# Branch stages of a first block run beside the next branch's projections, and modulation products moved into the merges

## What is computed

```python
# first block: four branches, merged
y_fox = attention(rms(q), rms(k), v, with a forget bias)         # 16 heads of 64
y_lru = rg_lru(proj("lru_x"), proj("lru_g"))                     # conv, gates, scan, gelu gate
y_sb  = stick_breaking_attention(q, k, v)                        # 16 heads of 64
y_mem = mem_attention(rms(q), rms(mem @ w_k), mem @ w_v)         # 4 heads of 256
gates = sigmoid(proj("gates") + b_gate)
mixed = sum_n gates_n * (y_n @ w_branch_n);  x = x + mixed @ w_out
# second block, each layer i
mod  = silu(c)     @ w_ada[i] + b_ada[i]                         # 6 vectors: shift, scale, gate, twice
modc = silu(c_ctx) @ w_ada[i] + b_ada[i]
h = modulate(rmsnorm(x, g1), sh1, sc1)                           # and the same for the context
ya, yb, yc = neighbourhood_attn, diff_attn, gmlp                 # layer 0: for x and for the context
m = ga * (ya @ w0) + gb * (yb @ w1) + gc * (yc @ w2)
x = x + gt1 * (m @ w_out);  then a mixture of 16 experts
```

## Time and profile before

| what | us |
|---|---|
| median of 3 runs (3232.24 to 3244.42) | 3238.53 |
| the profiled execution's own time | 3241.71 |
| its span, first to last instruction | 3239.9 |
| PE busy in it | 2658.2 |
| the stages fox, lru, sb projections, sb, memory projections together | 360.0 |
| the merge of the first block, the merge of layer 0 | 192.0, 199.1 |
| na_x, na_ctx, da_x of layer 0 together | 152.2 |

### The profile page before, as it was taken

The page is one execution under the profiler, slowest core; times in us unless marked ns, Lnnn a source line. Parts: engine busy times, 40 slices in busy tenths (PEclk is TensorE's granted clock), DMA queues, the critical chain, the costliest instruction groups (busy, mean ns, idle before and its releaser), DMA issues. The chain is left out here.

```text
span 3239.9 us, 36546 instructions
## 1 busy us (share of the span) xinstructions
PE 2658.2 (82%) x14364; PEld 1796.3 (55%) x14364; DVE 1169.5 (36%) x1596; ACT 882.3 (27%) x1314; POOL 39.9 (1%) x36
## 2 busy tenths in 40 slices
PE   6887898998998787889977778887887896787876
PEld 5666687998996464668753222223664894222222
DVE  4446544655753334344432001103444552000001
ACT  3344433544442232322221000002233432000001
POOL 0100000000000000000000000000000001000000
PEclk8888998999998898889978999998897997999999
DMA  4463532453542333112215999996211343999996
GB/s 154 157 257 113 198 130 92 178 185 123 188 159 91 150 136 130 50 69 100 85 46 224 404 405 407 403 414 260 78 52 50 142 165 147 413 410 409 411 410 269
DMA packets 92935, 669.19 MB, mean 207 GB/s; under 512 B 10320, under 2 KB 10496, under 8 KB 12800
## 3 DMA queue, kind: packets, MB, share of 16 engines
q1 hardware_dynamic: 90256, 654.67, 51.6%
q0 software_dynamic: 2272, 11.52, 1.0%
q10 hardware_dynamic: 272, 1.05, 0.1%
HBM read 666.13 MB, written 1.06 MB: 206 GB/s over the span
## 5 line engine op out<-in xcount | busy, mean ns | idle before, releaser
L1860 PE MATMUL ps<-ring,WK 128*64 128x512 f32 x3072 | 731.0, 605 | 171.2 <-DMA ring<-in_stream 147.1
L424 PE MATMUL ps<-A,piece_hi 128*128 128x256 f32 (+1 forms) x1952 | 618.5, 317 | 97.7 <-DVEq L358 33.1
L376 DVE TENSOR_TENSOR ring_lo<-ring,piece_hi 128x1024 fp32r<-128x1024 f32 x378 | 459.3, 1220 | 450.4 <-ACT piece_hi L369 449.3
L425 PE MATMUL ps<-A,piece_hi 128*128 128x256 f32 (+1 forms) x1952 | 612.5, 314 | 0.0
L426 PE MATMUL ps<-A,ring_lo 128*128 128x256 f32 (+1 forms) x1952 | 611.7, 313 | 0.0
L1860 PEld LDWEIGHTS ps<-ring,WK 128*64 128x64 f32 x3072 | 194.5, 137 | 674.2 <-DMA ring<-in_stream 371.9
L424 PEld LDWEIGHTS ps<-A,piece_hi 128*128 128x128 f32 x1952 | 384.7, 197 | 129.3 <-issue 59.2
L369 ACT ACTIVATE piece_hi<-ring 128x1024 fp32r<-128x1024 f32 x378 | 388.2, 1053 | 223.8 <-DVEq L450 131.9
L425 PEld LDWEIGHTS ps<-A,piece_hi 128*128 128x128 f32 x1952 | 385.6, 198 | 17.2
L426 PEld LDWEIGHTS ps<-A,ring_lo 128*128 128x128 f32 x1952 | 384.9, 197 | 18.1
L1980 DVE TENSOR_TENSOR WK<-WK,ps 128x512 f32<-128x512 f32 x32 | 22.0, 688 | 636.7 <-PE ps L1860 636.7
(11 more groups left out here) (252 smaller groups left out, 2447.6 us busy)
## 6 DMA issues: line engine op xcount, KB each, us to landing
ring<-in_stream SPq DMA_DIRECT2D x621, 1024.0 KB, 7.7
WK<-in_na_bias POOLq DMA_DIRECT2D x2, 2048.0 KB, 7.8
WK<-cum_scratch POOLq DMA_DIRECT2D x1, 2048.0 KB, 9.7
const<-in_const SPq DMA_DIRECT2D x1, 1267.0 KB, 11.7
WK<-in_x SPq DMA_DIRECT2D x1, 1024.0 KB, 5.4
WK<-in_mem SPq DMA_DIRECT2D x1, 1024.0 KB, 9.1
WK<-cum_scratch POOLq DMA_DIRECT2D x1, 1024.0 KB, 14.9
WK<-in_lru_w POOLq DMA_DIRECT2D x1, 1024.0 KB, 5.1
```

The costliest lines, as they stand in the source:

```text
L376: nc.vector.tensor_tensor(ring_lo[:, slot, at:at + PIECE], ring[:, slot, at:at + PIECE], f32(piece_hi[:, j, :]), ALU.subtract).then_inc(lo ...
L424: nc.tensor.matmul(out_, l[0], r[0], start=first, stop=False)
L425: nc.tensor.matmul(out_, l[0], r[1], start=False, stop=False)
L1860: last = nc.tensor.matmul(ps[64 * n:64 * n + 64, bank, :], lhs, piece[:, n * 512:n * 512 + 512], start=(k == 0), stop=(k == DC - 1))
```

## The change

**First block.** One projection bank (or a piece of v) stands behind each step of a round. The fox rounds carry the 16 banks of lru_x and lru_g; the recurrence carries the 24 pieces of the sb projections; the sb rounds carry the 16 banks of the memory branch's k and q; the stage of the sb projections is gone, with a barrier. The projections in rounds take PSUM banks 6 and 7 by turns (`set_ring`). The fox product moves from bank 6 to bank 4, the exponentials of round r + 1 stand behind the copy of round r, DVE's `probs(r + 1)` behind the split of a piece. The conv is done in the lru stage as before; Gelu is one operation over all 2048 columns.

**Modulation.** The groups leave the attentions. Each of the six is cut in two halves of 8 raw pieces, and a half stands in a merge, between the four banks of gates and the four banks of products: in halves 1 to 6 of the first block's merge, in all six of layer 0's. The merge uses banks 0 to 5, the modulation banks 6 and 7. The merges are written out, without a loop.

The diff, cut to its core:

```diff
+ADA_HALF = 8
+ADA_MERGE = {0: (1, 2, 3, 4, 5, 6), 1: (0, 1, 2, 3, 4, 5)}
@@ fox_pe
             scores(0)
             scores(1)
             for r in range(HEADS // 2):
+                turn(r)
+                also(2 * r)
+                product(r)
+                also(2 * r + 1)
                 if r + 2 < HEADS // 2:
                     scores(r + 2)
-                turn(r)
-                product(r)
-                after(r)
@@ fox_act
             for r in range(HEADS // 2):
-                if r + 1 < HEADS // 2:
-                    exps(r + 1)
                 act.wait_ge(att_turned, CREDIT + r + 1)
                 act.wait_ge(att_y, CREDIT + r)
                 nc.scalar.activation(fox_pt, ps[:, 4:6, 0:TRI], ACT.Copy).then_inc(att_copied, 1)
+                if r + 1 < HEADS // 2:
+                    exps(r + 1)
+                also(2 * r)
                 act.wait_ge(att_y, CREDIT + r + 1)
-                nc.scalar.activation(YT[:, 0, r, :], ps[:, 6, 0:T], ACT.Copy).then_inc(att_saved, 1)
-                after(r)
+                nc.scalar.activation(YT[:, 0, r, :], ps[:, 4, 0:T], ACT.Copy).then_inc(att_saved, 1)
+                also(2 * r + 1)
@@ sb_pe
             for r in range(SB_ROUNDS):
                 turn(r)
+                mem_piece_pe(pe, cur, 2 * r)
+                product(r)
+                mem_piece_pe(pe, cur, 2 * r + 1)
                 if r + 2 < SB_ROUNDS:
                     scores(r + 2)
-                product(r)
-                after(r)
@@ lru_pe
-            for c in range(DC):
-                pe.wait_ge(lru_xc, c + 1)
-                bank_parts(pe, cur, [... gates of chunk c ...])
+            for i in range(24):
+                sb_piece_pe(pe, cur, i)
+                if i < DC:
+                    if i == 0:
+                        pe.wait_ge(loads, 16 * LOADS["lru_w"])
+                    pe.wait_ge(lru_xc, i + 1)
+                    bank_parts(pe, cur, [(P, g * T, T, [(LW[:, g, i, :], LXC[:, i, :])]) for g in range(2)])
@@ lru_dve
+            for i in range(24):
+                if i < DC:
+                    lru_conv_dve(dve, steps, i)
...
+                sb_piece_read(dve, "dve", cur, i)
@@ merge_pe
                 for h in range(2):
+                    at = 2 * i + h
                     fm_banks(pe, cur, in_a()(n), n, 4)
+                    if ada is not None and ada_half(ada, at) is not None:
+                        ada_half_pe(pe, cur, ada, ada_half(ada, at))
+                    if ada is not None and ada_full_before(ada, at) is not None:
+                        ada_turn_pe(pe, 3 * ada + ada_full_before(ada, at) // 2)
                     if h == 0:
                         pe.wait_ge(y_lo, cur.base("y") + 1 + i)
                     fm_banks(pe, cur, lambda k: (yh[:, k, :], yl[:, k, :]), n, 4, kc)
@@ merge_dve, in a half
                     skip_fm(dve, cur, 4)
+                    if ada is not None and ada_half(ada, 2 * i + h) is not None:
+                        past_raw(dve, cur, ADA_HALF)
+                        if ada_half(ada, 2 * i + h) % 2 == 1:
+                            ada_rows_dve(dve, cur, ada, ada_half(ada, 2 * i + h))
@@
+        def ada_half_pe(pe, cur, layer, half):
...
+            for k in range(4 * (half % 2), 4 * (half % 2) + 4):
+                for q in range(4):
+                    if q % 2 == 0:
+                        piece = raw_piece(pe, cur)
+                        behind = cur.p - 1 - ADA_PIECE[layer, half]
+                        if behind < 4:
+                            pe.wait_ge(bank_free[cur.bank(cur.g - 4 + behind)], cur.bank_use(1, cur.g - 4 + behind))
+                    last = nc.tensor.matmul(ps[32 * q:32 * q + 32, b, :], CS[:, k, :], piece[:, ...], ...)
+                    if (k, q) == (DC - 1, 3):
+                        last.then_inc(ada_full, 1)
+                    elif q % 2 == 1:
+                        raw_used(last, cur)
@@ the program of PE; those of ACT and DVE alike
+            cur.set_ring((6, 7))
+            fox_pe(pe, cur, lambda i: fm_banks(pe, cur, in_a()(T), T, 1))
             barrier(pe, cur)
-            fm_banks(pe, cur, in_a()(T), T, 2 * DC)
+            cur.set_ring(range(NB))
             lru_pe(pe, cur)
             barrier(pe, cur)
-            qk_pe(pe, cur)
-            v_pe(pe, cur)
+            cur.set_ring((6, 7))
+            sb_pe(pe, cur)
             barrier(pe, cur)
-            sb_pe(pe, cur, ada_with_pe(pe, cur, "sb"))
-            barrier(pe, cur)
-            qk_pe(pe, cur, 0, T)
+            cur.set_ring(range(NB))
             head_norm_pe(pe, cur, mem_norm, between=lambda: v_pe(pe, cur, T))
```

More of the change, by code:

```diff
@@ L109, with merge_stretches @@
 RAW[PIECES:] = True
+ADA_HALF = 8
+ADA_MERGE = {0: (1, 2, 3, 4, 5, 6), 1: (0, 1, 2, 3, 4, 5)}
 ADA_PIECE = {}
[L112 to L122, removed]
+def merge_stretches(layer, halves, pieces):
+    out, k = [], 0
+    for h in range(halves):
+        out.append(4)
+        if h in ADA_MERGE[layer]:
+            out.append((layer, k))
+            k += 1
+        out.append(pieces - 4)
+    return out
+_at, _half = 0, {0: 8, 1: 6}
+for _n in ([(6 + 4 + 6 + 6) * 4] + merge_stretches(0, 8, _half[0]) + [BLOCK_PIECES - 22 * 4 - 8 * _half[0], 8 * 4]
+           + merge_stretches(1, 6, _half[1]) + [8, -EXPERTS * EXPERT_PIECES, MIX_PIECES, -EXPERTS * EXPERT_PIECES]):
+    if isinstance(_n, tuple):
+        ADA_PIECE[_n] = _at
+        _n = -ADA_HALF
+    RAW[_at:_at + abs(_n)] = _n < 0
+    assert _n > 0 or _n % 8 == 0
+    _at += abs(_n)
 assert _at == PIECES
@@ L136, in __init__ @@
         self.g = 0
+        self.places = []
+        self.ring = list(range(NB))
+        self.turn = 0
+        self.uses = [0] * NB
         self.i = None
@@ L1088, in fox_dve @@
             maxima(0)
+            probs(0)
             for r in range(HEADS // 2):
@@ L1091, in fox_dve @@
                     maxima(r + 1)
-                probs(r)
-                after(r)
+                also(2 * r)
+                if r + 1 < HEADS // 2:
+                    probs(r + 1)
+                also(2 * r + 1)
             fox_counts(cur)
@@ L1202, in sb_dve, with weights @@
                 nc.vector.memset(SB_B[r][:, :, SB - 1:SB], 0.0)
-            for r in range(SB_ROUNDS):
+            def weights(r):
                 W = SB_W[r % 3]
@@ new lines, in sb_piece_read, with op @@
+        def sb_piece_read(eng, who, cur, i):
+            if i < 2 * DC:
+                dst, scale = ((QT, HD ** -0.5), (KT, 1.0))[i // DC]
+                copies(eng, who, cur, lambda j: dst[:, j, :], 1, T, scale, first=i % DC)
+            elif i % 4 < 3:
+                next_piece(eng, cur)
+            else:
+                h = (i - 2 * DC) // 4
+                for j in range(TT):
+                    def op(bank, j=j):
+                        to = VT[:, j, h * 512:(h + 1) * 512]
+                        if who == "act":
+                            return nc.scalar.activation(to, bank, ACT.Copy)
+                        return nc.vector.tensor_copy(to, bank)
+                    read_bank(eng, cur, who == ("act", "dve")[j], op, piece=(j == TT - 1))
@@ L1286, in lru_dve @@
-            steps(nc.vector.tensor_tensor(LY, LXC[:, :, :], LG[:, :, :], ALU.mult))
-        def merge_loop(eng, cur, branches, kc, one_branch, steps=None, per=0):
-            if 2 * (4 + kc // 2) % (2 * R) == 0:
-                with loop(eng, cur, branches, pieces=2 * (4 + kc // 2), banks=16, steps=steps, steps_per=per) as i:
-                    one_branch(i)
-            else:
-                for i in range(branches):
-                    one_branch(i)
+            flat = lambda x: x.rearrange("p a t -> p (a t)")
@@ L1561, in gmod_dve, with ada_full_before @@
+        def ada_full_before(layer, at):
+            half = ada_half(layer, at - 1)
+            return half if half is not None and half % 2 == 1 else None
         def gmod_dve(dve, steps, g, which):
```

481 lines of the change are left out of this document (249 added, 232 removed).

## The result

| | us |
|---|---|
| before, median of 4 runs in the same comparison | 3235.39 (3227.95 to 3244.42) |
| after, median of 4 runs | 3287.71 (3281.58 to 3291.4) |
| ratio, with its 95% interval | 1.0159 (1.0127 to 1.0191) |
| span of the profiled execution, before and after | 3239.9, 3287.3 |

The changed kernel is slower by 1.6%, about 52 us. The forecast was 3293 us.

What follows compares the result with a forecast made beforehand. PE was taken to bound the kernel where full, chains elsewhere. The profiled 3241.7 - 65.5 (five stages) - 28 (layer 0's attentions) + 148 (merges) = 3296, lying 3.2 over the median, so 3293 us; range 3254 to 3324.

Steps and rivals of the forecast that it cites:

- The five stages: Fox to the memory projections: 294.5 us against 360.0, a gain of 65.5 (bounds 40 to 82).
- Fox: Fox stage: a chain through DVE's split sets rounds of 9.6 us, above PE's 8.5; stage 85 us.
- Lru: Lru stage with the sb projections: 75 us of PE plus 10.2 of waits and tail, 85 us (bounds 79 and 98).
- Layer 0's attentions: na_x, na_ctx and da_x lose their modulation: 11.3, 8.5 and 8.3 us, a gain of 28 (24 to 31).
- The merges: Both merges: 12 modulation halves at 9.95 + 2.2 us, plus 2 for exposed turns, a loss of 148 us.
- the 2 us for exposed turns: Merges: the turn of a finished group fits into the wait except once in each merge, 2 us for two.
- adds no work: Merges: writing the loop out adds no work to a full PE and was counted as nothing.
- Inside a half: Each merge half: PE idles 2.1 us for a landing, then 4.05 before products, which start 9.95 us after the gates.
- my term for the clock: Merges: lower granted clock after idle waits, 2.2 us per half (0 to 3.5), 26 us in all.
- Rival (a): Merges: the clock stays up, 12 x 2.2 us less, 3267 us, still slower; chance 0.18.
- Rival (b): Merges: the stream keeps up, a half costs only 3.64 us, total 3191 us, faster; chance 0.08.
- Rival (c): Fox, lru and sb: interleaved split, read and attention wait for each other, +13, +13 and +8, 3327 us; chance 0.12.

Runs made afterwards that it cites:

- e5_spread_fox: `e1_spread` with DVE's `probs` of the next round ahead of the split in fox; 3230.28 us, ratio 0.9988 to the kernel before.
- e4_fill: Changed kernel plus 28 unread products of 256 columns on PE between each half's modulation and its products; 3272.44 us.
- e6_none: Changed kernel without modulation products and their stream pieces, biases standing in, so part of the computation is left out; 3137.81 us.
- e7_lead: `e5_spread_fox` with one more piece split ahead behind the first three raw pairs of a half; 3192.24 us, ratio 0.9878 to the kernel before.
- e2_short_lead: `e1_spread`, but a raw piece counts as one of the three split ahead, as in the changed kernel; 3324.40 us.
- e1_spread: Changed kernel with two raw modulation pieces (one slot) behind every two merge banks, splits allowed to run past them; 3231.75 us.
- e3_four: Changed kernel with four raw pieces behind the gates and four behind the products, splits ahead as in `e1_spread`; 3231.14 us.
- e8_written_out: The kernel before, with only its first merge written out instead of looped; 3220.47 us, ratio 0.9974.

## Why the prediction was right

The time (3287.7 for 3293), the sign and the mechanism held. By its steps:

- **The five stages.** Forecast 65.5, measured 69.7. Fox 80.3 for 85: the round was 8.91 for 9.6, as the handovers and the bank's read that I estimated overlap in part; that the chain and not PE sets it is shown by `e5_spread_fox`. Lru 86.2 for 85, sb 79.5 for 79, memory 44.3 for 45.5. In lru two misses cancel: PE is busy 77.8 us where 75 were counted, and idles 8.4 where the waits were put at 10.2.
- **Layer 0's attentions.** 26.9 for 28: na_x 10.1, na_ctx 7.8, da_x 9.0.
- **The merges.** Loss 150 for 148; that these agree to 2 us is luck. The halves cost 12.7 and 13.1 us, not 12.15, 9 us more in all. Against that the loop gave 5 back, where "adds no work" to a full PE was taken for "nothing": that PE is busy 185.5 of 192.0 us meant that 6.5 were open, and I did not ask what released it there. And the 2 us for exposed turns are already in the 12.7 and 13.1.
- **Inside a half** the path was right and a little short. The wait for the landing is 2.4 us on average, for the split 3.8 and 4.4 (longest 5.1), where I had 2.1 and 4.05; from the first modulation product to the first product are 10.6 us on average in the first merge (10.0 to 11.4) and 11.0 in the other, against 9.95. What a half costs beyond that is 2.1 us in both merges, 26 us for twelve. That is the size of my term for the clock (26), which was carried over from a single gap in fox; `e4_fill` shows 20 of it directly, and the rest is not shown to be the clock.
- **Rival (a)**, the clock stays up, fell: PEclk 0.91 in both merges, and a gain by filler products alone. The Trainium skill (TensorE: Matmul & The Clock Gate, Part 1: The HAM clock gate) has the clock released by activity; the trace agrees, 1.00 in the merges of `e6_none` and 0.97 to 0.98 with products whose results nobody reads.
- **Rival (b)**, the stream keeps up, fell for this kernel, but its condition was the right one. In `e7_lead`, where each product piece is split in time, the kernel came to 3192; the rival had 3191, at 3.64 us a half and without the loop's and fox's gains. The half really costs 5.4, mostly for the reason in the last section. The Trainium skill (DMA: Bandwidth & Descriptors, Rules for kernel authors) wants a load issued early and waited for late; the trace agrees, 14.3 us of landing waits a merge with eight raw pieces in a row, none with two or four.
- **Rival (c)**, the interleaving binds beyond the forecast, fell: fox 80.3 where it had 98, lru 86.2 where it had 98, sb 79.5 where it had 87. What does bind, DVE's order in fox, was already in the forecast's 85 and is worth 3.6 us.

What the forecast left out is that the loss has two causes that can be parted. It priced the landing and the split as one chain. `e2_short_lead` has no burst and is slower than after; `e1_spread`, `e3_four` and `e7_lead` differ in how much is split in time.

## What to carry to other kernels

Work that uses up a ring of loads should be placed by the slot, not by the group: four slots used in 3.8 us cost 12 to 13 us each time, one slot at a time 5.4, if the splits run ahead over it; without that, one slot at a time cost more than the burst (14.6 and 17.2). Where pieces need a step of preparation, count how many prepared ones are left behind each foreign stretch, since eleven waits of 1.85 us cost 20 us and then another 14 by the lower clock. And in a fused loop, put what the attention's chain needs ahead of the filler work in each engine's program: here it was 0.5 us a round, 3.6 in all.

## What was not expected of the hardware

**A change of product kind has a price.** The end of a bank, a modulation pair and the next bank in `e1_spread`, where two products stand 0.23 us apart:

```profile
1350.89 0.39 PE L476 MATMUL ps<-A,ring_lo 128*128 128x512 f32 x1
1351.20 1.06 PE L1649 MATMUL ps<-ring,CS 128*32 128x512 f32 x8
1352.20 0.50 PE L474 MATMUL ps<-WKR,piece_hi 128*128 128x512 f32 x1
1352.54 0.39 PE L475 MATMUL ps<-WKR,piece_hi 128*128 128x512 f32 x1
```

From 1350.89 to 1352.54 are 1.65 us; two products would take 0.46, so the pair costs 1.19 and not the 0.91 that a quarter of the earlier trace rows gives. The starts show it: 0.31 and 0.34 where 0.23 is usual, and the first modulation product takes its share. In `e7_lead` a pair without a wait costs 1.2 us in both merges, so 24 pairs make 29 us of the 32 to 33 that it pays. Which of the differences (type, 32 columns for 128, the operands swapped) it is was not tried apart.

**Short waits took the clock down too, though not each time**: eight of the eleven waits of 1.85 us in `e1_spread` were followed by a granted clock between 0.50 and 0.66, while the similar waits of up to 1.7 us in `e3_four` left it at 0.99 to 1.00 over the whole merges, and the 24 waits of 1.6 us in `e2_short_lead` took its first merge to 0.93. What decides it is open.

**A loop's turn cost PE about 1 us** in the first merge of before, where nothing else held PE but one wait of 1.4 us (`e8_written_out`).
